# A hybrid attention layer on one core: the first two tiles as a pair per piece of weights, their 1/rms rows turned on TensorE, ScalarE's table loaded up front

## The reference, cut to what matters

```python
xn   = rms_norm(x, norm_in)                    # x: (1, 2048, 1024), float32
proj = einsum('bsd,dn->bsn', xn, w_in)         # 1024 x 2464
a_q, a_k, a_v, a_g, b_cq, b_ckv, b_kr, b_g = split(proj)
q, k = rope(rms_norm(a_q)), rope(rms_norm(a_k))          # 8 heads of 64, 2 key heads
y_a  = attention(q, k, a_v)
qb   = einsum(rms_norm(b_cq), w_uq)                      # latent of 384 -> 4 heads of 96
kvb  = einsum(rms_norm(b_ckv), w_ukv)                    # latent of 256 -> 4 x (64 + 128)
qb, kb = rms_norm and rope(qb), rms_norm and rope([k_nope, b_kr])
y_b  = attention(qb, kb, vb)
out  = x + einsum([y_a * silu(a_g), y_b * silu(b_g)], w_out)
```

## Time and profile before

| | us |
|---|---|
| median of 3 runs | 1655.33 (1654.47 to 1655.79) |
| profiled execution | 1650.56 |
| its span | 1648.7 |
| TensorE busy | 1527.9 (93%) |
| VectorE busy | 1165.7 (71%) |
| ScalarE busy | 1053.7 (64%) |
| GpSimd busy | 582.5 (35%) |

### The profile page before, as it was taken

How to read it: one execution, slowest core, us unless ns; L and a number is a source line. 1 busy time by engine, 2 the same in 40 slices (tenths; PEclk the granted TensorE clock), 3 DMA queues, 4 the chain that set the end, 5 groups by cost and what they waited for, 6 DMA issues and landing times. The chain is left out here.

```text
span 1648.7 us, 36763 instructions
## 1 busy us (share of the span) xinstructions
PE 1527.9 (93%) x13136; PEld 878.3 (53%) x13136; DVE 1165.7 (71%) x1616; ACT 1053.7 (64%) x1377; POOL 582.5 (35%) x508
## 2 busy tenths in 40 slices
PE   2889999999993699999999999999999999949999
PEld 1345555555551356665666566556655665634444
DVE  4754646465554889889988998899889988743332
ACT  5644544444441588888888888888888888841110
POOL 0100000000000356656665666566666666710000
PEclk9999999999996799999999999999999999979999
DMA  9547555755556532423232333223332433179994
GB/s 243 179 93 163 143 130 138 165 141 119 143 114 141 162 64 62 97 68 70 64 80 64 75 77 80 63 66 90 80 63 60 96 78 65 41 185 239 245 238 119
DMA packets 354831, 189.77 MB, mean 115 GB/s; under 512 B 174561, under 2 KB 335713, under 8 KB 354785
## 3 DMA queue, kind: packets, MB, share of 16 engines
q1 hardware_dynamic: 329088, 173.25, 43.4%
q10 hardware_dynamic: 24672, 14.88, 3.6%
q0 software_dynamic: 1024, 1.06, 0.5%
HBM read 119.22 MB, written 40.93 MB: 97 GB/s over the span
## 5 line engine op out<-in xcount | busy, mean ns | idle before, releaser
L950 POOL TENSOR_TENSOR p_pl<-p_p,p_ph 128x512 f16<-128x512 f32 x384 | 502.2, 1314 | 406.3 <-ACT p_ph L986 347.5
L1001 DVE TENSOR_REDUCE p_part<-p_mx 128x2 f32<-128x1024 f32 x384 | 468.3, 1220 | 85.9 <-PE p_mx L1077 67.6
L977 ACT ACTIVATE p_p<-p_st 128x1024 f32<-128x1024 f32 x384 | 391.0, 1018 | 124.7 <-PE p_st L1109 68.4
L678 PE MATMUL p_ring<-p_w_hi,p_xT 128*128 128x512 f16 (+3 forms) x1536 | 386.5, 339 | 34.9 <-ACT p_w_hi L450 29.1
L986 ACT ACTIVATE p_ph<-p_p 128x1024 f16<-128x1024 f32 x336 | 355.2, 1057 | 18.3
L1029 DVE TENSOR_TENSOR p_pl<-p_p,p_ph 128x512 f16<-128x512 f32 x384 | 325.6, 848 | 9.3 <-ACT p_ph L986 8.5
L678 PE MATMUL p_ring<-p_w_lo,p_xT 128*128 128x512 f16 (+3 forms) x768 | 260.3, 339 | 0.0
L678 PEld LDWEIGHTS p_ring<-p_w_hi,p_xT 128*128 128x128 f16 x1536 | 151.0, 98 | 155.7 <-DVE p_xT L549 29.1
L1141 PE MATMUL p_acc<-p_vas,p_ph 128*128 128x129 f16 x2048 | 207.9, 221 | 0.0
L1142 PE MATMUL p_acc<-p_vas,p_pl 128*128 128x65 f16 x2048 | 201.0, 193 | 0.0
L1141 PEld LDWEIGHTS p_acc<-p_vas,p_ph 128*128 128x128 f16 x2048 | 180.6, 97 | 36.4 <-issue 14.3
(11 more groups left out here) (114 smaller groups left out, 1904.4 us busy)
## 6 DMA issues: line engine op xcount, KB each, us to landing
p_vbs<-scratch_vb SPq DMA_DIRECT2D x16, 1028.0 KB, 6.2
p_xin<-in_x SPq DMA_DIRECT2D x16, 512.0 KB, 6.0
p_xcol<-in_x_cols SPq DMA_DIRECT2D x16, 512.0 KB, 5.9
scratch_g<-p_g SPq DMA_DIRECT2D x16, 512.0 KB, 3.6
p_kb<-scratch_kb SPq DMA_DIRECT2D x32, 256.0 KB, 5.2
p_xr<-in_x SPq DMA_DIRECT2D x16, 512.0 KB, 4.4
out<-p_res SPq DMA_DIRECT2D x16, 512.0 KB, 3.1
p_gt<-scratch_g ACTq DMA_DIRECT2D x14, 512.0 KB, 4.6
```

The costliest lines, as they stand in the source:

```text
L678: last = pe.matmul(ring_t[:, 0:w], a, b, start=(k == 0 and m == 0), stop=(k == len(steps) - 1 and m == len(terms) - 1))
L950: pool.tensor_tensor(pl[:, s % NP, 1, :], p32[:, s % N32, QB:], ph[:, s % NP, 1, :], ALU.subtract).then_inc(s_lop, 1)
L977: act.activation(p32[:, s % N32, :], st[:, s % 2, :, :].rearrange("p a b -> p (a b)"), ACT.Exp, scale=scale).then_inc(s_exp, 1)
L1001: dve.tensor_reduce(part[:, e // MPAIRS % 3, 2 * c:2 * c + 2], mx[:, :, :], AX, ALU.max).then_inc(s_red, 1)
```

## The change

The first pair gets an order of its own on each engine (first_pair). TensorE runs both tiles' cq and ckv, then both tiles' aq, then the rest alternately, so that each piece of weights is used by two tiles soon after its split; the ring of banks follows a list (FIRST). cq32 and ckv32 are doubled, one for each tile. The 1/rms rows of tiles 0 and 1 come from TensorE: a float32 transpose of the column, broadcast, against an identity matrix that is a new input (eye), into a PSUM bank of its own (rsp), which x_scale reads; GpSimd spreads from tile 2 on. ScalarE's first instruction is a Sqrt of one column. SP issues the identity and x's columns ahead of cq's weights, and x(2) and the last two pieces behind turn_latents(0). From the third tile on the order is as before; some waits are given in other counts (GpSimd waits for the store's completion as before). GpSimd's fills, its wait for all splits and its four clears stay.

The diff, cut to its core; the functions that ScalarE's and VectorE's first_pair call (cq_out, ckv_out, latent_stat, latent_hi, aq_out, akv_out, up_out, heads_sq, v_hi, heads_dev; latent_rstd, latent_lo, heads_sum, v_lo, heads_chain) are the former tile body in pieces; a split with 0 or 1 is the first or second half of a piece, split_all is both.

```diff
         sb = lambda n, s, d=F32: ctx.enter_context(nc.sbuf_tensor("p1_" + n, s, d))
...
         lstat = sb("lstat", [P, 2, 8])
         junk = sb("junk", [P, D])
         xT = sb("xT", [P, 2, 2, KT, P], F16)
-        cq32 = sb("cq32", [P, RQ])
...
         ring = [ps(f"ring{i}", [P, 512]) for i in range(3)]
-
-        s_const = sem("const_loaded")
+        rsp = ps("rsp", [P, 2, P])
+
+        s_gin = sem("input_gain_loaded")
+        s_eye = sem("eye_loaded")
+        s_const = sem("latent_gains_loaded")
+        s_rsp = sem("rstd_rows_in_psum")
...
+        FIRST = [(0, "cq"), (0, "ckv"), (1, "cq"), (1, "ckv"), (0, "aq"), (1, "aq"), (0, "akv"), (0, "uq"), (0, "ukv0"), (0, "ukv1"),
+                 (1, "akv"), (0, "ag"), (1, "uq"), (1, "ukv0"), (1, "ukv1"), (0, "bg"), (1, "ag"), (1, "bg")]
+
         def turn(t, name):
 
+            if early_x(t):
+                return FIRST.index((t, name))
             if isinstance(t, int) and t >= T14:
...
-            sp.dma_start(xin[:, :], xt[0]).then_inc(s_x, 16)
-            sp.dma_start(gin[:, :], g_in.rearrange("l (k p) -> (l p) k", p=P), allow_slow_non_contiguous=True).then_inc(s_const, 16)
-            sp.dma_start(gcq[:, :], g_cq.rearrange("l (k p) -> (l p) k", p=P), allow_slow_non_contiguous=True).then_inc(s_const, 16)
-            sp.dma_start(gckv[:, :], g_ckv.rearrange("l (k p) -> (l p) k", p=P), allow_slow_non_contiguous=True).then_inc(s_const, 16)
-            for n in range(len(pieces)):
+            def load_cols(t):
+
+                if t > 0:
+                    sp.wait_ge(s_xt, t)
+                sp.dma_start(xcol[:, :, :], x_cols[t]).then_inc(s_xc, 16)
+
+            def load_w(n):
                 raw, src, gain, hi, lo = pieces[n]
                 if turns[n] > 0:
...
                     sp.wait_ge(s_wlo, rows_before[before + 1])
                 for b in range(2):
                     sp.dma_start(raw[:, half(n, b), :], src[:, half(n, b), :]).then_inc(s_w[slots[n]][b], 16)
-                if n == 0:
-                    sp.dma_start(xcol[:, :, :], x_cols[0]).then_inc(s_xc, 16)
-                if n == 1:
-                    load_x(1)
-                if n == 3:
-                    load_x(2)
-                if n == 4:
-                    sp.wait_ge(s_xt, 1)
-                    sp.dma_start(xcol[:, :, :], x_cols[1]).then_inc(s_xc, 16)
-                if n == 6:
-                    sp.dma_start(trg[:, 0, :], trt[0]).then_inc(s_trig[0], 16)
-                    sp.dma_start(gains[:, :], g_heads.partition_broadcast(P)).then_inc(s_gains, 16)
-
...
+            def first_pair():
+                sp.dma_start(xin[:, :], xt[0]).then_inc(s_x, 16)
+                sp.dma_start(gin[:, :], g_in.rearrange("l (k p) -> (l p) k", p=P), allow_slow_non_contiguous=True).then_inc(s_gin, 16)
+                sp.dma_start(eye32[:, :], eye).then_inc(s_eye, 16)
+                load_cols(0)
+                load_w(0)
+                load_x(1)
+                load_w(1)
+                sp.dma_start(gcq[:, :], g_cq.rearrange("l (k p) -> (l p) k", p=P), allow_slow_non_contiguous=True).then_inc(s_const, 16)
+                sp.dma_start(gckv[:, :], g_ckv.rearrange("l (k p) -> (l p) k", p=P), allow_slow_non_contiguous=True).then_inc(s_const, 16)
+                load_w(2)
+                load_w(3)
+                load_cols(1)
+                load_w(4)
+                load_w(5)
+                turn_latents(0)
+                load_x(2)
+                load_cols(2)
+                load_w(6)
+                load_trig(0)
+                load_trig(1)
+                sp.dma_start(gains[:, :], g_heads.partition_broadcast(P)).then_inc(s_gains, 16)
+                load_x(3)
+                load_w(7)
+                turn_latents(1)
+                store_v(0)
+                load_x(4)
+                store_v(1)
+                store_g(0)
+                turn_z(0)
+                load_cols(3)
+                store_g(1)
+
+            def tile(i, h, last):
...
-                if not (last and h == 1):
-
-                    if not (first and h == 0):
-                        sp.wait_ge(s_rc, t * RC)
-                    sp.dma_start(trg[:, 1 - h, :], trt[t + 1]).then_inc(s_trig[1 - h], 16)
+                if t == 2:
+                    sp.wait_ge(s_rc, RC)
+                    load_trig(2)
+                if t + 1 < TILES:
+                    sp.wait_ge(s_rc, t * RC)
+                    load_trig(t + 1)
                 turn_latents(t)
                 if t + 3 < TILES:
...
             eng.wait_ge(s_dx, t + 1)
             eng.dma_start(RS[t], stat[:, t % 2, 2:3]).then_inc(s_rs, 16)
-            eng.wait_ge(s_rs, t * 16 + 16)
-            if t > 1:
+            eng.wait_ge(s_rs, t * 16 - 16)
+            if t > 3:
                 eng.wait_ge(s_xs, t - 1)
             eng.dma_start(rsb[:, t % 2, :], RS[t].partition_broadcast(P)).then_inc(s_rsb[t % 2], 16)
...
-            spread_rstd(pool, 0)
-            spread_rstd(pool, 1)
...
-                if not early_x(t):
-                    act.wait_ge(s_rs, t * 16 - 16)
+                if not (isinstance(t, int) and t < 4):
+                    act.wait_ge(s_rs, t * 16 - 48)
...
+            def first_pair():
+                act.wait_ge(s_eps, 1)
+                act.activation(stat[:, 0, 7:8], eps[:, :], ACT.Sqrt)
+                x_stat(0, 0)
+                act.wait_ge(s_gin, 16)
+                split_hi(0, 0)
+                x_hi(0, 0)
+                split_hi(0, 1)
+                x_stat(1, 1)
+                split_all(1)
+                cq_out(0, 0)
+                act.wait_ge(s_const, 32)
+                split_all(2)
+                x_hi(1, 1)
+                ckv_out(0, 0)
+                latent_stat(0, 0)
+                split_all(3)
+                split_hi(4, 0)
+                latent_hi(0, 0)
+                cq_out(1, 1)
+                split_hi(4, 1)
+                ckv_out(1, 1)
+                latent_stat(1, 1)
+                x_stat(2, 0)
+                split_all(5)
+                aq_out(0, 0)
+                split_hi(6, 0)
+                aq_out(1, 1)
+                latent_hi(1, 1)
+                split_hi(6, 1)
+                akv_out(0, 0)
+                split_hi(7, 0)
+                up_out(0, 0)
+                heads_sq(0, 0)
+                v_hi(0)
+                split_hi(7, 1)
+                heads_dev(0)
+                akv_out(1, 1)
+                gate(0, "ag")
+                x_stat(3, 1)
+                up_out(1, 1)
+                heads_sq(1, 1)
+                v_hi(1)
+                gate(0, "bg")
+                x_hi(2, 0)
+                heads_dev(1)
+                z_hi(0, 0)
+                gate(1, "ag")
+                gate(1, "bg")
...
-                dve.wait_ge(s_rsb[h], (t - h) * 8 + 16)
-                dve.tensor_tensor(xcol[:, :, :], xcol[:, :, :], rsb[:, h, :].unsqueeze(1).to_broadcast([P, KT, P]),
-                                  ALU.mult).then_inc(s_xs, 1)
+                if early_x(t):
+                    dve.wait_ge(s_rsp, t + 1)
+                    rows = rsp[:, t, :]
+                else:
+                    dve.wait_ge(s_rsb[h], (t - h) * 8)
+                    rows = rsb[:, h, :]
+                dve.tensor_tensor(xcol[:, :, :], xcol[:, :, :], rows.unsqueeze(1).to_broadcast([P, KT, P]), ALU.mult).then_inc(s_xs, 1)
...
-            loop(dve, lambda i, first, last: [tile(i, h, first, last) for h in range(2)])
+            def first_pair():
+                dve.memset(eps[:, :], EPS).then_inc(s_eps, 1)
+                x_rstd(0, 0)
+                x_scale(0, 0)
+                dve.wait_ge(s_gin, 16)
+                split_lo(0, 0)
+                x_lo(0, 0)
+                split_lo(0, 1)
+                x_rstd(1, 1)
+                split_all(1)
+                x_scale(1, 1)
+                dve.wait_ge(s_const, 32)
+                split_all(2)
+                x_lo(1, 1)
+                latent_rstd(0, 0)
+                split_all(3)
+                split_lo(4, 0)
+                latent_lo(0, 0)
+                split_lo(4, 1)
+                latent_rstd(1, 1)
+                x_rstd(2, 0)
+                split_all(5)
+                split_lo(6, 0)
+                latent_lo(1, 1)
+                split_lo(6, 1)
+                split_lo(7, 0)
+                heads_sum(0)
+                v_lo(0)
+                split_lo(7, 1)
+                heads_chain(0, 0)
+                x_rstd(3, 1)
+                x_scale(2, 0)
+                heads_sum(1)
+                v_lo(1)
+                z_lo(0, 0)
+                x_lo(2, 0)
+                heads_chain(1, 1)
...
+            def rstd_rows(t):
+
+                pe.wait_ge(s_dx, t + 1)
+                pe.transpose(rsp[:, t, :], stat[:, t, 2:3].to_broadcast([P, P]), eye32[:, :]).then_inc(s_rsp, 1)
...
+            def first_pair():
+                pe.wait_ge(s_eye, 16)
+                rstd_rows(0)
+                pe.wait_ge(s_xt, 1)
```

(97 more changed lines are left out.)

180 lines of the change are left out of this document (89 added, 91 removed).

## The result

The changed kernel took 1634.55 us in the median (1634.26 to 1635.33, 4 runs), the kernel before 1655.56 us beside it; the ratio is 0.9868, 95% interval 0.9849 to 0.9887. It is 21.0 us faster. Later on, one execution of each kernel fell in a slow state (1815.3 us before, 5342.7 us changed); both are left out of every median and ratio here.

What follows compares the result with a forecast made beforehand. TensorE, busy without a break from tile 2's start at 107.9 us, was taken as the bound; that start at 92.1 and 2.9 us of half clock gave a gain of 13.1 us: 1642.2 us, range 1635.5 to 1649.5.

Steps and rivals of the forecast that it cites:

- slow stretch: Loads at 14 to 16 us, stream at 58 GB/s before; left open whether it stays or goes with the store.
- slow and fast case: Stage one's pair if the slow stretch stays (last split 67.5, gain 10.4 us) or goes (62.4, gain 15.5 us).
- What bounds the kernel, and the quantity to predict: Stage one: TensorE runs without a break from tile 2's first matmul (107.9 us), so that moment was to be predicted.
- First matmul: Start of stage one: TensorE begins at 12.5 us instead of 29.13, 16.6 us sooner, but this is not the gain.
- X and E: The pair: ScalarE's x_stat(2) starts at X = 45.3 (fast 40.2); VectorE's last split ends at E = 67.5 (62.4).
- From E to tile 2: After the last split: 19.0 us through clears, store and spread to x_scale(2), then 8.1 to tile 2's start.
- TensorE's own chain: The pair's matmuls on TensorE end at 87.5 us (fast 82.4), 7 us before tile 2 starts.
- The half clock: Tile 2's start after the idle time: TensorE's clock is down as after the earlier gap, costing 2.9 us.
- A: GpSimd's store and spread through DRAM get shorter with fewer loads under way: gain 20 us, 1635; chance 0.13.
- B: SP's queue feeds the pair's loads too late: gain 3 to 9 us, about 1649; chance 0.20.
- C: Nothing is left in the pair: x_stat(2) starts at about 53, gain 2.7 us, 1652.6; chance 0.06.
- D: ScalarE's order in the pair becomes the bound through a second wait before "bg": 4.7 us slower, 1660; chance 0.04.

Runs made afterwards that it cites:

- experiment 4: The changed kernel with two GpSimd stores of 128 times 4 bytes to DRAM put back, read by nobody: 1644.27 us, ratio 0.9932 to the kernel before.
- experiment 5: The changed kernel with two spare stores: 64 KB in 512-byte rows from GpSimd's queue, 1631.02 us; 128 times 4 bytes from SP's queue, 1641.27 us.

## Why the prediction was low

The forecast went wrong at one step, the slow stretch of the loads, and was low in several sizes besides. Step by step against it (slow and fast case as it named them):

- *What bounds the kernel, and the quantity to predict.* Right. The end of stage one moved with tile 2's start: 107.9 to 87.13 is 20.8 us, less 1.8 us of half clock, 19.0.
- *First matmul.* Forecast 12.5, it was 13.52; the weights' first half landed at 9.1 instead of 8.0. The turn took 0.45 us (6.10), under the 1 us taken, and x_scale with its operand in PSUM 1.22 us, where it took 1.23 us from SBUF before.
- *The slow stretch.* This is the step that failed. I left it open whether the 58 GB/s stretch hung on the 4-byte store, and took the middle of the two gains, 10.4 and 15.5 us (that is 12.95; the 13.1 is a slip of 0.15). Experiments 4 and 5 show that it did, so the fast case (15.5 us) was the forecast to make. The stretch was also priced too low: 5.1 us between the two cases, while it cost 6.6 us of stage one when experiment 4 put it back. The kernel before had a second sign that I had not used: there too the stream was slow again (111 GB/s at 30 to 32 us, at a DMA share of 1.13) after the second store was issued at 22.3 us. The other steps are sizes within the fast case:
- *X and E.* x_stat(2) started at 36.92, not 40.2: the two turns held SP's queue 1.32 + 1.26 us, not 2.91 + 2.59, and xin(2) landed sooner. (The forecast has SP issue x's columns of tile 2 ahead of the turns before the change; the trace has them behind, at 54.87 against 48.65. No term rests on it. Its 45.3 and 40.2 for X should be 45.5 and 39.9 by its own issue times plus 5.) From there to the last split it was 23.9 instead of 22.2 us, with one wait that I had excluded: 1.62 us for "bg"'s first half. E was 60.86 against 62.4.

```profile
30.30 1.32 SPq L349 DMA_TRANSPOSE p_latT<-p_lat_hi  x1
31.68 1.26 SPq L351 DMA_TRANSPOSE p_latT<-p_lat_lo  x1
```

- *From E to tile 2.* Forecast 19.0 + 8.1, measured 18.57 + 7.7. Right, and so was what stood behind it: GpSimd's order. TensorE's own chain ended at 81.8 (82.4 in the fast case), so it idled for 5.30 us and not for 7.
- *The half clock.* I took the 2.9 us of the old gap, behind which the granted clock was 0.50 until 102. Here it lasted from 87.13 to about 90.6 (0.86 in the mean of 90 to 92) and so cost 1.8 us: 1.1 us too much.

The sum: 15.5 + 1.5 (E) + 0.4 + 0.4 (road) + 1.1 (clock) = 18.9, against 19.0 measured for stage one. Of the miss of 7.9 us, 2.4 lie in taking the middle instead of the fast case, 3.4 in these sizes, and about 2 outside stage one, which is open. The slow stretch is the largest single term. But the time missed the range by only 0.95 us; had any one of the terms from 1.1 us up been right, forecast and range would have moved by more than that. The forecast set its median by subtracting the gain from 1655.33, which is right in principle, but with a stage three that moves by 6 us a range should have carried some 2 us more on each side for that alone.

*The rivals.* A (a shorter road) didn't happen: the store waited 7.75 us and the spread took some 5.5. Its figures (a gain of 20 us, 1635) are the nearest to what was measured, but by coincidence, since its mechanism isn't there. The Trainium skill (DMA: Bandwidth & Descriptors, "Anatomy of one DMA") puts a DMA at about 2 us plus its bytes; the traces had 7.75 us here and 10 to 13 us among loads for 512 bytes. The same page's section "Specifications" says that transfers below 512 bytes are done by read-modify-write; that fits experiment 5, where 512-byte rows did no harm and 4-byte ones did, though no run here shows what the write does inside. B, C and D didn't happen: SP's new order held nothing up but 1.97 us before x_stat(2) and 1.62 us before "bg"'s first half. The table: 1.28 us at 0.74 and one only, as said; its gain is nothing that the runs can tell, as said (1633.26 us without it, 1634.55 with it).

## What to carry to other kernels

Look for small writes to DRAM in a stretch that is bound by loads: here 512 bytes in 4-byte pieces took 10 to 13 us to land, and from 12 to 20 us 1.0 MB came in where 3.1 MB did beside the wide stores. That cost stands in no engine's busy time. It shows in the GB/s of the stretch, at a DMA share that still looks busy (0.77 and 1.08 in experiments 4 and 5), and in the landing times of others. A value that only has to change its layout between partitions and rows went over TensorE in 0.45 us instead. And when a change has two parts, price each with the other absent: the pair order is a gain only once the stores are gone, and moving a store "earlier, off the critical road" can put it where it does harm.

## What the runs showed of the hardware

- A store of 128 times 4 bytes among weight loads of about 400 GB/s pulled the stream down to 58 to 198 GB/s for 6 to 10 us, from GpSimd's queue and from SP's alike (10.2 to 11.4 us to landing on the one, 13.0 to 13.4 on the other); two stores of 64 KB in 512-byte rows landed in 5.3 us and left it at 321 to 414 GB/s from 12 to 20 us. Behind the second small store the GB/s alone say less, because SP has few loads to issue there in the kernel without stores too (28 to 124 GB/s at 28 to 34 us).
- The float32 turn of a broadcast column (128x128) took 0.45 us on TensorE from idle, and VectorE read the rows from PSUM in 1.22 us for 1024 columns, the time that it needed from SBUF (1.23).
- Stage three of this kernel takes 177.5 to 184.1 us from one execution to the next with unchanged code, while stages one and two repeat within 1 us. Between its shortest and its longest, a wait of 5.71 us for a DMA and the lower granted clock (0.97 against 0.99 in the mean) make the difference; why the DMA was late is open.
